# Feed-forward of the second layer: one weight load for the rounded features and their rest

## The reference, cut to what matters

```python
def _swiglu(h, p):
    gate, up = jnp.split(h @ p['w_gu'], 2, axis=-1)      # w_gu (1024, 2 x 2816)
    return (jax.nn.silu(gate) * up) @ p['w_down']        # w_down (2816, 1024)
...
    x = x + g2 * _swiglu(_modulate(_rmsnorm(x, p['norm2_g']), sh2, sc2), p)
    if last:
        return x, None
...
    return _rmsnorm(x, final_g)
```

## Time and profile before

| | |
|---|---|
| median of 3 runs | 1277.47 us (1276.66 to 1277.97) |
| the profiled execution | 1277.61 us |
| its span, first to last instruction | 1275.8 us |
| mean granted TensorE clock | 0.988 of 2.4 GHz |
| TensorE / VectorE / ScalarE busy | 1216.1 / 781.1 / 521.4 us |
| layer 1 feed-forward in the span | about 1073.9 to 1267.4 us |

### The profile page before, as it was taken

The page is one execution under the profiler, slowest core; times in us unless marked ns, Lnnn a source line. Parts: engine busy times, 40 slices in busy tenths (PEclk is TensorE's granted clock), DMA queues, the critical chain, the costliest instruction groups (busy, mean ns, idle before and its releaser), DMA issues. The chain is left out here.

```text
span 1275.8 us, 17575 instructions
## 1 busy us (share of the span) xinstructions
PE 1216.1 (95%) x7212; PEld 987.8 (77%) x7212; DVE 781.1 (61%) x1273; ACT 521.4 (41%) x903; POOL 1.8 (0%) x8
## 2 busy tenths in 40 slices
PE   5999999999999899999999999999988998999998
PEld 3666777777676687788888888668778687999997
DVE  5653347867866654587655556555589876555554
ACT  4353445442444433222223322446565354443444
POOL 0000000000000000000000000000000000000000
PEclk9999999999999899999999999999999999999999
DMA  9833244441111243455555554323334223555653
GB/s 338 275 115 128 69 159 137 133 148 50 34 34 34 67 115 96 148 193 186 186 181 177 198 190 152 87 66 100 99 105 127 67 51 109 185 184 183 182 171 127
DMA packets 132456, 171.89 MB, mean 135 GB/s; under 512 B 9332, under 2 KB 112406, under 8 KB 132376
## 3 DMA queue, kind: packets, MB, share of 16 engines
q1 hardware_dynamic: 131892, 170.58, 41.6%
q10 hardware_dynamic: 484, 0.18, 0.1%
HBM read 169.69 MB, written 1.05 MB: 134 GB/s over the span
## 5 line engine op out<-in xcount | busy, mean ns | idle before, releaser
L1697 DVE TENSOR_TENSOR w_lo<-w_raw,w_hi 128x1024 fp32r<-128x1024 f32 (+1 forms) x220 | 264.2, 1204 | 234.1 <-ACT w_hi L1338 233.1
L1338 ACT ACTIVATE w_hi<-w_raw 128x1024 fp32r<-128x1024 f32 (+1 forms) x220 | 228.6, 1042 | 398.1 <-DMA w_raw<-in_w_gu_dram 184.9
L680 PE MATMUL ps<-h_hi,w_hi 128*128 128x512 f32 (+1 forms) x896 | 310.6, 347 | 2.8 <-DVE qk L1884 1.7
L682 PE MATMUL ps<-h_hi,w_lo 128*128 128x512 f32 (+1 forms) x896 | 303.8, 339 | 0.0
L681 PE MATMUL ps<-h_lo,w_hi 128*128 128x512 f32 (+1 forms) x896 | 303.7, 339 | 0.0
L680 PEld LDWEIGHTS ps<-h_hi,w_hi 128*128 128x128 f32 x896 | 170.6, 190 | 33.1 <-issue 15.4
L680 PE MATMUL ps<-f_hi,w_hi 128*128 128x512 f32 (+1 forms) x544 | 188.0, 346 | 5.7 <-DVE att_lo L2232 2.7
L682 PEld LDWEIGHTS ps<-h_hi,w_lo 128*128 128x128 f32 x896 | 170.5, 190 | 18.9
L681 PEld LDWEIGHTS ps<-h_lo,w_hi 128*128 128x128 f32 x896 | 170.8, 191 | 17.3
L682 PE MATMUL ps<-f_hi,w_lo 128*128 128x512 f32 (+1 forms) x544 | 182.9, 336 | 0.0
L681 PE MATMUL ps<-f_lo,w_hi 128*128 128x512 f32 (+1 forms) x416 | 139.9, 336 | 0.0
(11 more groups left out here) (312 smaller groups left out, 1610.3 us busy)
## 6 DMA issues: line engine op xcount, KB each, us to landing
w_raw<-in_w_gu_dram SPq DMA_DIRECT2D x88, 512.0 KB, 3.6
w_raw<-in_w_in_dram SPq DMA_DIRECT2D x60, 512.0 KB, 3.9
m_raw<-in_w_mod_dram SPq DMA_DIRECT2D x32, 512.0 KB, 5.0
w_raw<-in_w_down_dram SPq DMA_DIRECT2D x32, 512.0 KB, 3.9
m_even<-in_w_mod_dram SPq DMA_DIRECT2D x12, 1024.0 KB, 5.8
m_odd<-in_w_mod_dram SPq DMA_DIRECT2D x12, 1024.0 KB, 5.9
m_first<-in_w_mod_dram SPq DMA_DIRECT2D x16, 512.0 KB, 10.5
w_raw<-in_w_out_dram SPq DMA_DIRECT2D x16, 512.0 KB, 3.4
```

The costliest lines, as they stand in the source:

```text
L680: mm(o, w_hi[:, i % RING, w], hi[:, 0:n], start=first and k == 0, stop=False)
L682: last = mm(o, w_lo[:, i % RING, w], hi[:, 0:n], start=False, stop=final and k == nk - 1)
L1338: A(w_hi[:, i % RING, w], w_raw[:, i % RING, w], ACT.Copy).then_inc(w_hi_done, 1)
L1697: TT(w_lo[:, i % RING, w], w_raw[:, i % RING, w], w_hi[:, i % RING, w].bitcast(F32), ALU.subtract).then_inc(w_lo_done, 1)
```

## The change

In layer 1 the 256 columns of the rounded features and the 256 of their rest are streamed in one matmul of 512 columns against `w_hi`, into the two halves of the bank; `w_lo` x hi is added to the first half as before. So a weight tile has two matmuls and two weight loads in place of three. This holds for gate, up and the column pieces 0 to 2 of down; the fourth stays as it was. Whoever reads the bank now adds its halves: for gate and up VectorE does so with a tensor_reduce over groups of two into `gate` and `hidden` in SBUF, and Silu and the product work on these; `residual` applies a second scalar_tensor_tensor to the upper half. Besides, two pairs of start-up semaphores are merged.

```diff
+def whole(l, ch):
+    return l == 1 and ch < 3
...
-        h_hi, h_lo = at("h_hi", 16, [KD, T], F32R), at("h_lo", 32, [KD, T], F32R)
+        h_both = at("h_both", 16, [2, KD, T], F32R)
+        h_hi, h_lo = h_both[:, 0], h_both[:, 1]
...
+            def both_of(i, q, j, nk, both, first, final):
+                o = ps[:, 2 * (q % 2) + j, :]
+                for k in range(nk):
+                    w = slice(k * CW + j * P, k * CW + (j + 1) * P)
+                    mm(o.rearrange("p (a t) -> p a t", a=2), w_hi[:, i % RING, w], both(k), start=first and k == 0, stop=False)
+                    last = mm(o[:, 0:L], w_lo[:, i % RING, w], both(k)[:, 0, :], start=False, stop=final and k == nk - 1)
+                return last
+            def h_of(half):
+                return lambda k: h_both[:, :, 4 * half + k, 0:L]
...   (h_pair)
+                                if n == L:
+                                    mm(ps[:, b + j, :].rearrange("p (a t) -> p a t", a=2), w_hi[:, s, w],
+                                       h_both[:, :, 4 * half + k, 0:L], start=(half == 0 and k == 0), stop=False)
...   (gate and up on TensorE, l == 1)
+                                both_of(i, q, 0, 4, h_of(half), half == 0, half == 1)
+                                both_of(i, q, 1, 4, h_of(half), half == 0, half == 1).then_inc(w_used, 1)
...   (down on TensorE)
+                                if whole(l, ch):
+                                    last = both_of(i, q0 + ch, j, k1 - k0, lambda k: f_both[:, :, k0 + k, 0:L], sub == 0, sub == 2)
...   (hidden_high on ScalarE)
-                    act.wait_ge(pair_free[q % 2], q // 2 + 1)
+                    if l == 0:
+                        act.wait_ge(pair_free[q % 2], q // 2 + 1)
+                    else:
+                        p.after("hidden_ready")
...   (Silu)
+                                    act.wait_ge(pair_free[q % 2], q // 2 + 1)
+                                    p.sig(A(gate[:, :, 0:n], gate[:, :, 0:n], ACT.Silu), "gate_ready")
...   (residual)
+                    if stage != "out" and whole(l, ch):
+                        p.chain(ins)
+                        ins = STT(out=res, in0=ps[:, 2 * (q % 2) + jj, L:2 * L],
+                                  scalar=modv[:, l, gate_blk + blk, 0:1], in1=res, op0=ALU.mult, op1=ALU.add)
...   (VectorE)
+                def add_halves(dst, q, used):
+                    dve.wait_ge(w_used, used)
+                    src = ps[:, 2 * (q % 2):2 * (q % 2) + 2, :].rearrange("p j (a t) -> p j t a", a=2)
+                    V.tensor_reduce(out=dst[:, :, 0:L], in_=src, op=ALU.add, axis=AX_X).then_inc(pair_free[q % 2], 1)
...   (hidden_full)
+                    if l == 1:
+                        add_halves(hidden, q + 1, g0 + 4 * f + 4)
+                        dve.wait_ge(pair_free[(q + 1) % 2], (q + 1) // 2 + 1)
+                        p.after("gate_ready")
+                        p.sig(TT(hidden[:, :, 0:n], hidden[:, :, 0:n], gate[:, :, 0:n], ALU.mult), "hidden_ready")
+                        p.own("hidden_ready")
+                        return
...   (loop over r, after split_w and hidden_low)
+                            if l == 1 and r == (3 if (part, f) == (0, 0) else 2):
+                                add_halves(gate, q0 + 2 * f, g0 + 4 * f + r)
```

More of the change, by code:

```diff
@@ L253, in backbone @@
         st = at("st", 180, [2, 512])
-        f_hi, f_lo = at("f_hi", 88, [12, T], F32R), at("f_lo", 112, [12, T], F32R)
+        f_both = at("f_both", 88, [2, 12, T], F32R)
+        f_hi, f_lo = f_both[:, 0], f_both[:, 1]
         att_lo, hy_lo = at("att_lo", 156, [4, T], F32R), at("hy_lo", 164, [4, T], F32R)
@@ L730, in h_pair @@
                                 w = slice(k * CW + j * P, k * CW + (j + 1) * P)
-                                mm(o, w_hi[:, s, w], hi, start=(half == 0 and k == 0), stop=False)
-                                mm(o, w_hi[:, s, w], lo, start=False, stop=False)
+                                if n == L:
+                                    mm(ps[:, b + j, :].rearrange("p (a t) -> p a t", a=2), w_hi[:, s, w],
+                                       h_both[:, :, 4 * half + k, 0:L], start=(half == 0 and k == 0), stop=False)
+                                else:
+                                    mm(o, w_hi[:, s, w], hi, start=(half == 0 and k == 0), stop=False)
+                                    mm(o, w_hi[:, s, w], lo, start=False, stop=False)
                                 last = mm(o, w_lo[:, s, w], hi, start=False, stop=(half == 1 and k == 3))
@@ L862, in at_piece @@
                     if s == S_DT:
-                        p.after("dt_rows")
-                        if l == 0:
-                            p.after("dsel_ready")
+                        p.after("dt_rows", 2 - l)
                         for t in range(4):
@@ L1219, in _ @@
                                 pair_open(q)
-                            block_of(i, q, 0, 4, n, h_blocks(half), half == 0, half == 1)
                             if l == 0:
+                                block_of(i, q, 0, 4, n, h_blocks(half), half == 0, half == 1)
                                 mods_in_ffn(ffn_slot(part, 4 * f + r))
-                            block_of(i, q, 1, 4, n, h_blocks(half), half == 0, half == 1).then_inc(w_used, 1)
+                                block_of(i, q, 1, 4, n, h_blocks(half), half == 0, half == 1).then_inc(w_used, 1)
+                            else:
+                                both_of(i, q, 0, 4, h_of(half), half == 0, half == 1)
+                                both_of(i, q, 1, 4, h_of(half), half == 0, half == 1).then_inc(w_used, 1)
                     g0, q0 = PLAN[l, f"down{part}"]
@@ L1234, in _ @@
                             for j in range(2):
-                                last = block_of(i, q0 + ch, j, k1 - k0, n, lambda k: (f_hi[:, k0 + k, :], f_lo[:, k0 + k, :]),
-                                                sub == 0, sub == 2)
+                                if whole(l, ch):
+                                    last = both_of(i, q0 + ch, j, k1 - k0, lambda k: f_both[:, :, k0 + k, 0:L], sub == 0, sub == 2)
+                                else:
+                                    last = block_of(i, q0 + ch, j, k1 - k0, n, lambda k: (f_hi[:, k0 + k, :], f_lo[:, k0 + k, :]),
+                                                    sub == 0, sub == 2)
                                 if (ch, sub, j) == (3, 2, 0):
@@ L1338, in round_w @@
                     A(w_hi[:, i % RING, w], w_raw[:, i % RING, w], ACT.Copy).then_inc(w_hi_done, 1)
-            p.after("eps_ready")
+            p.after("consts_set")
             act.preload_act_table_set("natural_log_exp_and_others")
@@ L1349, in _ @@
             p.chain(A(vecT[:].rearrange("p l v -> p (l v)"), ps[:, 6, 0:DEPTH * NV], ACT.Copy))
-            p.after("cact_cleared")
+            p.after("consts_set")
             A(cact[:, :, 0], vecT[:, 0, V_C:V_C + 8], ACT.Silu)
@@ L1627, in _ @@
                                 q = q0 + 2 * f
-                                act.wait_ge(w_used, g0 + 4 * f + r)
-                                A(gate[:, :, 0:n], ps[:, 2 * (q % 2):2 * (q % 2) + 2, 0:n], ACT.Silu).then_inc(pair_free[q % 2], 1)
+                                if l == 0:
+                                    act.wait_ge(w_used, g0 + 4 * f + r)
+                                    A(gate[:, :, 0:n], ps[:, 2 * (q % 2):2 * (q % 2) + 2, 0:n], ACT.Silu).then_inc(pair_free[q % 2], 1)
+                                else:
+                                    act.wait_ge(pair_free[q % 2], q // 2 + 1)
+                                    p.sig(A(gate[:, :, 0:n], gate[:, :, 0:n], ACT.Silu), "gate_ready")
                     g0, q0 = PLAN[l, f"down{part}"]
@@ L1774, in add_final @@
                         p.own("square_added")
-            p.sig(V.memset(eps1[:, 0:1], EPS), "eps_ready")
-            p.sig(V.memset(cact[:], 0.0), "cact_cleared")
+            p.sig(V.memset(eps1[:, 0:1], EPS), "consts_set")
+            p.sig(V.memset(cact[:], 0.0), "consts_set")
             dve.wait_ge(sq_full, 16)
@@ L1803, in _ @@
                     dve.wait_ge(sq_full, 16)
-                    p.sig(TT(dsel[0:32, :], ident[0:32, 0:16], ident[0:32, 16:32], ALU.add), "dsel_ready")
+                    p.sig(TT(dsel[0:32, :], ident[0:32, 0:16], ident[0:32, 16:32], ALU.add), "dt_rows")
                     for k in range(KD):
```

5 lines of the change are left out of this document (3 added, 2 removed).

## The result

The changed kernel takes 1280.49 us (median of 13 runs, 1279.08 to 1282.96) against 1277.47 for the kernel before on the same chip: a ratio of 1.0025, 95% interval 1.0014 to 1.0035. Run once more on another chip it gave 1282.20 against 1278.05, ratio 1.0031 (1.0017 to 1.0044). So it is slower by some 3 to 4 us. The forecast was 1278.9, 1.4 us above the kernel before: the sign of the sum was right, its size half of what came, within the range. The difference of 0.24% lies just outside the 0.2% that the forecast called no difference (chance 0.48), in the outcome "slower" that it gave 0.30.

A forecast was written before the change was run, and what follows sets the result against it. TensorE's matmul pitch was taken as the bound. From the profiled 1277.61 us: -6.1 + 2.1 + 1.6 + 1.0 + 0.7 + 2.1 = +1.4, 1279.0; that execution being 0.14 above the median, 1278.9, range 1273.5 to 1283.4.

The forecast's parts named there:

- 479 x 12.7 ns = 6.1 us saved: TensorE, second layer's feed-forward: 479 weight tiles at 346.4 ns (226.7 + 119.7) instead of 0.3591 us, 6.1 us saved.
- A: First gate: TensorE's block 1 waits for VectorE's split of piece 5, then the gate sum; 2.1 us added.
- B: Behind the first gate: some 2.5 us idle drops the clock to 0.50 for 3.4 us; 1.6 us added.
- The rival that nothing much is saved: Weight tiles: a matmul's fixed part hardly counts, so 1.2 us saved in place of 6.1, total 1283.8; chance 0.05.
- The rival "the clock holds": Behind the first gate: the clock does not drop, 1.6 us less, total 1277.3; chance 0.22.
- C: Blocks of part 2: VectorE's gate sum and Silu delay later rounding and splits; 1.0 us added over 4 blocks.
- D: Last block before part 2's down product: the same chain with 768-element pieces makes TensorE wait; 0.7 us added.
- E: Part 2's down product: ScalarE's scaling waits for the longer residual, delaying rounding; stalls of 1.45 and 0.7, together 2.1 us.
- Sums over pairs: VectorE's sums of gate and up halves, 1024 elements into 512: taken as 1.22 us each.
- the rival of 1.75: VectorE's gate and up sums take 1.75 us each, 4.5 us more, total 1283.4; chance 0.12.
- The rival of few waits: Queues give way less, later waits and the clock drop come to nothing: total 1273.5, faster; chance 0.19.

The follow-up runs named there:

- Experiment 11: Changed kernel with the w_lo matmuls also run over all 512 columns, so that no width alternates: 1327.43 us (one run).
- Experiment 1: Changed kernel with VectorE's sum of the gate halves put ahead of the split of the same step: 1278.68 us, ratio 0.9999 to the kernel before.
- experiment 2: Changed kernel with 18 unused 256-column matmuls ahead of the first gate's wait: 1279.66 us, ratio 1.0010 to the kernel before.
- 3: Changed kernel with rounded features and their rest side by side, one run of 512 columns for gate and up: 1280.49 us, ratio 1.0017 to the kernel before.
- 4: Changed kernel with two 512-wide matmuls, then two 256-wide ones, in place of alternating widths: 1281.00 us, ratio 1.0023 to the kernel before.
- Experiment 5: Changed kernel with ScalarE's finishing copies in part 2's down product moved behind the next rounding: 1279.03 us, ratio 1.0007 to the kernel before.
- experiment 6: Changed kernel with the down product of part 2 back to 256-wide matmuls as in the kernel before: 1279.32 us, ratio 1.0012 to the kernel before.
- 7: Changed kernel with the gate's sum ahead of the split and the finishing copies one step later: 1275.89 us, ratio 0.9985 to the kernel before.
- experiment 8: Changed kernel with gate's sum first, finishing copies later, and eight 512-wide matmuls ahead of eight 256-wide ones: 1274.47 us, ratio 0.9975 to the kernel before.
- 10: Repeat of experiment 8's kernel, on the chip where the changed kernel was run again: 1275.60 us, ratio 0.9981 to the kernel before.
- experiment 9: The changed kernel run again unaltered, on another chip: 1282.20 us, ratio 1.0031 to the kernel before.

## Why the prediction was right or wrong

From the last matmul of the first block (1086.82 and 1085.58) to that of the last down piece (1267.12 and 1269.06) the kernel before took 180.30 us and the changed one 183.48: 3.18 more. The first block itself had won 0.31, which leaves 2.87 in all. The forecast's sum was 1.4. (The two executions as wholes differ by 2.04 only, since what comes before this feed-forward happened to be shorter in the second.)

- **The gain per tile: the step that failed.** "479 x 12.7 ns = 6.1 us saved" added the pitches of two streams of one width each. Experiment 11 gives 226.6 for the wide stream with the new operands, so that part was right. But in alternation the two take 353 to 354 ns for most of the time and 346 to 347 for the rest. The old tile was a little too small as well: 0.3591 covers twelve rows only, 0.3600 the feed-forward. So 6.6 ns were saved for most of the time where 12.7 were counted. The waits below add up to 6.6 us and the whole to 2.87, which leaves a gain of 3.7 us of the 6.1. The 19 pieces between the two load issues say the same: 0.81 us shorter, with 0.6 of waits in them, is 1.4 of gain where 1.93 was due. The rival that nothing much is saved fell too: the matmul's fixed 13 ns is real, as the earlier trace rows had it, and half of it was lost again.
- **A, the first gate.** Forecast 2.1. From the first block's last matmul to the next one's first went 3.34 us (1085.58 to 1088.92) against 0.72: 2.6. The order of the queues was right; the load of piece 5 took 5.07 us to land instead of 4.45, and ScalarE's rounding waited 0.27 for it. Experiment 1 shows the cause: 1.4 us are the split ahead of the sum, the rest is the sum.
- **B, the clock.** Forecast 1.6 from two cases; 1.5 by experiment 2. At this gate it fell with each idle time of 2.9 us and more (the changed kernel twice, experiments 3 to 6 and 11) and with none of 2.0 and less (1, 2, 7, 8, 10). The rival "the clock holds" was wrong for this kernel and right for the mended one.
- **C, blocks of part 2.** Forecast 1.0. Three pieces took 0.19, 0.14 and 0.28 more than their neighbours: 0.6. In the second execution, whose loads landed in 3.5 us, none did (experiment 9), and experiment 6 ties the waits to the slow loads within one trace. That the landing time decides was in the forecast, that it differs between executions was not. For part 1 the forecast had no wait; the first execution has none, but the second had 0.4 us, and the traces of experiments 3 and 4 had 0.8 and 1.1. A load issued near 1107 had landed there in 4.5, 4.6 and 5.2 us.
- **D, ahead of the down product of part 2.** Forecast 0.7; 0.5, and in experiment 6 again; nothing in the second execution (experiment 9). It hangs on slow loads as C does.
- **E, in that product.** Forecast 1.45 + 0.7 = 2.1; pieces 6 and 9 took 4.64 and 3.60 where 3.53 and 3.31 had been, together 1.4 more. The first of the two stalls was a little shorter than forecast (a wait of 1.11; residual 1.90 as taken), the second 0.3. Experiment 5 shows the cause.
- **Sums over pairs.** 1.22 taken, 1.216 measured; the rival of 1.75 fell.

Put together, the forecast counted 2.4 us too much gain and 0.5 too little for A, against 1.3 too much for C, D and E and 0.1 for B: 1.5 us low in the trace, 1.6 by the medians. That it came so near is in part luck, since errors of opposite sign met, and C and D were there in this execution and not in the next. The rival of few waits was partly right about C, D and E, and never near its sum, since A and B alone took 4.1.

What isn't settled is why mixed widths cost more. Known is that the excess is 7 ns a tile or nothing when they alternate, taken up at a restart, and steadily 2 to 3 ns when they are grouped by two or by eight.

## What to carry to other kernels

Where two kinds of matmul are to be mixed, take the pitch from a row of the mixture, not from the sum of two pure streams, and read each over a hundred tiles or more; without such a row, let the range hold the whole saving as doubtful. When work moves onto the path between a bank and its reuse, put it at the head of its engine's queue: here the same change went from 0.25% slower to 0.15% faster by moving one sum and one copy. And idle time that a change adds is to be priced with the clock drop that can stand behind it: here 1.5 us on top of 2.6. A term that hangs on when a load lands is to be taken from several executions, since one trace shows only one case.

## What the runs showed of the hardware

- A stream of matmuls of 512 and 256 columns in turn runs at 346 to 347 or at 353 to 354 ns a pair, in one kernel and in one execution; the changes came at waits or between stages. Streams of one width kept one value, 227 ns for 512 columns and 120 for 256.
- With eight of one width behind eight of the other (experiment 8) the first five wide ones took 228 to 236 ns and the last three 227, the first narrow one 113 and the others 119 to 120.
- Idle times at the same place of 1.7 to 2.0 us left the granted clock at 1.00, behind ones of 2.9 to 3.9 us it stood at 0.50 (1.2 GHz) for 3.4 or 6.8 us.
- Loads of 512 KB in the same part of the same kernel landed in 4.6 us (median) in one execution and in 3.5 in another; in experiment 6 they went from 3.5 to 4.5 in the middle of the part.
- Summing groups of two from PSUM on VectorE takes 1.216 us for 1024 elements, no more than a subtraction of as many in SBUF (1.224).
